# Between two stages of a three-block transformer kernel: where the next weights are split, how the last tiles are normed, and where the gate row and the meta tokens stand

## The reference

```python
# block 0 and 1 (the mixer is attention+convolution in 0, a 2-D Fourier transform in 1)
u = layer_norm(h) * (1 + sc1) + sh1
y = mixer(u) @ w_out
h = layer_norm(ALPHA * h + g1 * y) * ln_g[0] + ln_b[0]
u = layer_norm(h) * (1 + sc2) + sh2
h = layer_norm(ALPHA * h + g2 * (relu(u @ w1)**2 @ w2)) * ln_g[1] + ln_b[1]
# block 2 (16 learned meta tokens ahead of the 1024)
h = concat([meta_tokens, h])
h = h + mixer2(rmsnorm(h) * g) @ w_out_2
h = h + relu(rmsnorm(h) * g @ w_up)**2 @ w_down
return (rmsnorm(h) * final_g)[16:]
```

## Time and profile before

| | before |
|---|---|
| median of 3 runs | 3486.8 us (3484.27, 3486.8, 3490.0) |
| the profiled execution | 3484.21 us, span 3482.0 us, 2.2 us outside the span |
| mean granted TensorE clock | 0.958 of full speed |
| PE matmul busy | 3177.9 us, 91% of the span |
| DVE, ACT, POOL busy | 2156.8 us (62%), 1387.6 us (40%), 1074.6 us (31%) |
| chain that ended last | PE 72%, DVE 15%, ACT 8%, issue 3%, DMA 1% |

### The profile page before, as it was taken

The page is one execution under the profiler, slowest core; times in us unless marked ns, Lnnn a source line. Parts: engine busy times, 40 slices in busy tenths (PEclk is TensorE's granted clock), DMA queues, the critical chain, the costliest instruction groups (busy, mean ns, idle before and its releaser), DMA issues.

```text
span 3482.0 us, 36701 instructions
## 1 busy us (share of the span) xinstructions
PE 3177.9 (91%) x14623; PEld 2620.0 (75%) x14623; DVE 2156.8 (62%) x2795; ACT 1387.6 (40%) x1951; POOL 1074.6 (31%) x485
## 2 busy tenths in 40 slices
PE   7999888779999999869799999997985899999997
PEld 3888777668888888667588888886864678888886
DVE  4624677565777776775565666656776665555554
ACT  4311687344333333341533333335355353333332
POOL 0001464134444441322243344411580022222220
PEclk9999999989999999989899999998987899999999
DMA  6435211211233332110111111121120011111111
GB/s 220 141 128 159 77 55 35 85 42 61 98 103 103 102 102 75 33 37 19 43 55 49 55 49 49 49 67 32 37 92 18 25 55 60 50 61 49 55 55 55
DMA packets 190996, 237.86 MB, mean 68 GB/s; under 512 B 9672, under 2 KB 149563, under 8 KB 190827
## 3 DMA queue, kind: packets, MB, share of 16 engines
q1 hardware_dynamic: 173338, 172.90, 15.9%
q0 software_dynamic: 9136, 32.22, 2.5%
q10 hardware_dynamic: 8352, 30.41, 2.4%
HBM read 218.70 MB, written 16.79 MB: 68 GB/s over the span
## 4 chain that ended last, share of the span: by engine, by line
PE 72%; DVE 15%; ACT 8%; issue 3%; DMA 1%; SPq 0%; POOL 0%; DVEq 0%; ACTq 0%; POOLq 0%
PE psum L607 23%; PE psum L608 23%; PE psum L609 23%; DVE small L738 2%; DVE page_r L618 2%; DVE small L1367 2%; ACT temp L909 2%; DVE H L1472 1%; ACT U_hi L613 1%; DVE PT_lo L618 1%; DMA page<-in_ada_w_dram 1%; ACT prob L1333 1%; ACT page_r L613 1%; PE psum L899 1%; DVE small L763 1%
## 5 line engine op out<-in xcount | busy, mean ns | idle before, releaser
L607 PE MATMUL psum<-U_hi,page_r 128*128 128x512 f32 x2108 | 837.3, 397 | 62.6 <-DVE page_r L618 39.0
L608 PE MATMUL psum<-U_lo,page_r 128*128 128x512 f32 x2108 | 830.1, 394 | 0.0
L609 PE MATMUL psum<-U_hi,page_r 128*128 128x512 f32 x2108 | 829.3, 393 | 0.0
L618 DVE TENSOR_TENSOR page_r<-page,page_r 128x1024 fp32r<-128x1024 f32 (+2 forms) x239 | 350.9, 1475 | 371.9 <-ACT page_r L613 369.5
L607 PEld LDWEIGHTS psum<-U_hi,page_r 128*128 128x128 f32 x2108 | 402.0, 191 | 156.9 <-DVE page_r L618 42.8
L613 ACT CAST page_r<-page 128x1024 fp32r<-128x1024 f32 (+2 forms) x323 | 336.7, 1047 | 400.3 <-DVE page L638 110.1
L1972 ACT ACTIVATE temp<-psum 128x512 f32<-128x512 f32 x192 | 114.7, 598 | 884.6 <-PE psum L609 840.5
L609 PEld LDWEIGHTS psum<-U_hi,page_r 128*128 128x128 f32 x2108 | 401.6, 191 | 85.3
L608 PEld LDWEIGHTS psum<-U_lo,page_r 128*128 128x128 f32 x2108 | 402.3, 191 | 81.6
L607 PE MATMUL psum<-page_r,act_page_r 128*128 128x512 f32 x1176 | 457.5, 389 | 0.0
L608 PE MATMUL psum<-page_r,act_page_r 128*128 128x512 f32 x1176 | 457.5, 389 | 0.0
(11 more groups left out here) (344 smaller groups left out, 4849.7 us busy)
## 6 DMA issues: line engine op xcount, KB each, us to landing
page<-in_mlp_w_dram SPq DMA_DIRECT2D x128, 512.0 KB, 4.1
page<-in_ada_w_dram SPq DMA_DIRECT2D x48, 512.0 KB, 4.9
page<-in_w_in_dram SPq DMA_DIRECT2D x38, 512.0 KB, 4.1
page<-in_w_up_dram SPq DMA_DIRECT2D x32, 512.0 KB, 4.1
page<-in_w_down_dram SPq DMA_DIRECT2D x32, 512.0 KB, 4.3
ada_land<-in_ada_w_dram ACTq DMA_DIRECT2D x24, 512.0 KB, 4.4
sum_page<-in_ada_w_dram ACTq DMA_DIRECT2D x12, 512.0 KB, 5.5
act_page<-in_ada_w_dram ACTq DMA_DIRECT2D x12, 512.0 KB, 8.6
```

Of the source, the lines that this page charges most:

```text
L607: pe.matmul(out, l_hi, r_hi, start=start, stop=False, skip_group_check=read_between)
L608: pe.matmul(out, l_hi, r_lo, start=False, stop=False, skip_group_check=read_between)
L609: return pe.matmul(out, l_lo, r_hi, start=False, stop=stop, skip_group_check=read_between)
L618: return dve.tensor_tensor(lo, src, hi.bitcast(F32), ALU.subtract).then_inc(*k.lo.inc(*key))
```

## The change

It has six parts. (1) `place_mlp_unit`: u1, u2, u3 of an MLP's block 0 land in pages 0, 1, 2 and not in their slots' lo pages. d0 to d2, which land in the same pages, now wait for the splits of u1 to u3. (2) The splits of those weights (and of weights 2 to 4 of the projection behind `post3`), which stood behind or ahead of the whole late norm chain, are spread through it: `units(1)`, `units(2)`, `units(3)`. (3) The norm of tiles 6 and 7 in the four boundaries with a post norm is two steps on DVE, (h - mean) * g and then * scale + b, with no ACT instruction; the first of them for tile 6 and the second measuring of tile 5 move among the `U_lo` of chunk 0. (4) The gate rows (0,1) and (1,1) move from the MLP's block 0 to the place between the two halves of the output product before it, and all gate rows use a spread tile with four eighths side by side, so that DVE no longer waits for PE between eighths. (5) Two steps on one element per partition (L745 and L763) become `tensor_scalar` with per-partition scalars, from `scalar_tensor_tensor` with two tensors. (6) The norm of the meta tokens moves ahead of the projection's first tile, their transposes behind (3,0).

```diff
@@ place_mlp_unit
-        u.page = lo
-        u.raw = self.page[:, lo].rearrange("p a n -> p (a n)")
-        u.left_by = left[lo]
+        early = what == "u" and blk == 0 and j > 0
+        u.page = j - 1 if early else lo
+        u.raw = self.page[:, u.page].rearrange("p a n -> p (a n)")
+        u.left_by = left[u.page]
+        if early:
+            left[u.page] = [("taken", u)]
@@ dve_gate_row
     on.wait_ge(*k.lo.now())
+    if (layer, which) != (0, 0):
+        on.wait_ge(*k.gate_turned.at(*((layer, 0) if which else (layer - 1, 1)), KT - 1))
     for i in range(KT):
-        if i >= 2:
-            on.wait_ge(*k.gate_turned.at(layer, which, i - 2))
-        dve.tensor_scalar(k.temp[3 + i % 2][:, 0:P], k.ones[:], k.mod[:, layer, col + i:col + i + 1], None,
-                          ALU.mult).then_inc(*k.gate_spread.inc(layer, which, i))
+        dve.tensor_scalar(k.temp[3 + i // 4][:, (i % 4) * P:(i % 4 + 1) * P], k.ones[:],
+                          k.mod[:, layer, col + i:col + i + 1], None, ALU.mult).then_inc(
+            *k.gate_spread.inc(layer, which, i))
@@ dve_measure, dve_scale
-        m = dve.scalar_tensor_tensor(s[0:rows, 13:14], s[0:rows, 12:13], s[0:rows, 12:13], s[0:rows, 13:14], ALU.mult,
-                                     ALU.add)
+        m = dve.tensor_scalar(s[0:rows, 13:14], s[0:rows, 12:13], s[0:rows, 12:13], s[0:rows, 13:14], ALU.mult, ALU.add)
-        m = dve.scalar_tensor_tensor(s[:, 14:15], s[:, 12:13], -1.0, s[:, 15:16], ALU.mult, ALU.mult)
+        m = dve.tensor_scalar(s[:, 14:15], s[:, 12:13], s[:, 15:16], -1.0, ALU.mult, ALU.mult)
@@ pe_mix_out (and the same in pe_fourier; spreads and copies on DVE and ACT to match)
+    pe_gate_row(k, pe, on, 0, 1)
     for tt in range(TT):
         pe_down_tile(k, pe, on, "mix1", tt, units[FB:], lambda j, tt: u_operands(k, 4, j, tt),
@@ class Boundary
+    def late_units(self, k, n):
+
+        if self.name == "post3":
+            at = k.first["in2"]
+            return {1: (), 2: (at + 2,), 3: (at + 3, at + 4)}[n]
+        return (k.first[{"post0": "mlp0", "post2": "mlp1", "pre4": "mlp2"}[self.name]] + n,)
@@ act_boundary, at the last tile
+    units(1)
+    if b.rows:
+        act_root(k, act, on, P, b.name, "post", TT - 1)
+        act_root(k, act, on, P, b.name, "pre", TT - 3)
+        units(2)
+        act_root(k, act, on, P, b.name, "pre", TT - 2)
+    for t in range(TT - 3 if not b.from_u else TPC, TT - 1):
+        hat(t)
+    act_root(k, act, on, P, b.name, "pre", TT - 1)
+    hat(TT - 1)
+    if not b.rows:
+        units(2)
+    units(3)
@@ dve_boundary
+    def gain(t):
...
+        dve.scalar_tensor_tensor(h, h, mean, k.row_g[:], ALU.subtract, ALU.mult).then_inc(*k.step.inc())
+        on.wait_ge(*k.step.now())
+        dve.scalar_tensor_tensor(h, h, scale, k.row_b[:], ALU.mult, ALU.add).then_inc(*k.dve_gained.inc(b.name, t))
...
+    def between(i):
+
+        if b.rows and i == 0:
+            gain(TT - 2)
+        if b.rows and i == 4:
+            measure("pre", TT - 3)
...
+    units(1)
+    if b.rows:
+        measure("post", TT - 1)
+        units(2)
+        measure("pre", TT - 2)
+        scale("post", TT - 1)
+        gain(TT - 1)
+        scale("pre", TT - 3)
+        scale("pre", TT - 2)
+    measure("pre", TT - 1)
+    hat(TT - 3)
+    scale("pre", TT - 1)
+    hat(TT - 1)
+    if not b.rows:
+        units(2)
+    units(3)
@@ pe_mixers
         if (m, c) == (3, 0):
+            pe_boundary_rest(k, pe, on, b)
+        if (m, c) == (0, 1):
             on.wait_ge(*k.hat_ok.at("meta"))
```

More of the change, by code:

```diff
@@ L547, in place_mlp_unit @@
         self.parts_at(u, hi, lo)
-        u.before = [("product", (name, blk - 1), "6")] if blk and (what, j) == ("u", 1) else left[hi]
+        u.before = [("product", (name, blk - 1), "6")] if blk and (what, j) == ("u", 1) else left[hi] + (left[lo] if early else [])
         left[hi] = left[lo] = [("done", u.s)]
@@ L1515, in act_mix_out @@
         act_weights(k, act, on, k.first["mix"] + n)
+    act_gate_row(k, act, on, 0, 1)
     for tt in range(TT):
         act_boundary(k, act, on, BOUNDARY[0], tt)
-    for n in range(9, 12):
-        act_weights(k, act, on, k.first["mix"] + n)
 def dve_mix_out(k, dve, on):
@@ L1658, in turn, with units @@
             hat(old)
-    turn(tt)
+    def units(n):
+        for s in b.late_units(k, n):
+            act_weights(k, act, on, s)
+    if tt < TT - 1 or b.fourier:
+        turn(tt)
     if tt == TT - 2 and b.fourier:
@@ L1681, in dve_boundary, with measure, scale, hat @@
 def dve_boundary(k, dve, on, b, tt):
+    def gain(t):
+        h = k.H[:, t, :]
+        mean, scale = k.small[:, k.smalls.of(b.name, "post", t), 12:13], scale_bias(k, P, True, b.name, "post", t)[0]
+        on.wait_ge(*k.scaled.at(b.name, "post", t))
+        on.wait_ge(*k.row_g_in.at(b.name))
+        on.wait_ge(*k.row_b_in.at(b.name))
+        dve.scalar_tensor_tensor(h, h, mean, k.row_g[:], ALU.subtract, ALU.mult).then_inc(*k.step.inc())
+        on.wait_ge(*k.step.now())
+        dve.scalar_tensor_tensor(h, h, scale, k.row_b[:], ALU.mult, ALU.add).then_inc(*k.dve_gained.inc(b.name, t))
+    def measure(which, t):
+        if which == "pre":
+            on.wait_ge(*b.gained(k, t))
+        else:
+            on.wait_ge(*k.h_added.at(b.down, t, 1))
+        dve_measure(k, dve, on, k.H[:, t, :], P, D, b.rms if which == "pre" else False, b.name, which, t)
+    def scale(which, t):
+        dve_scale(k, dve, on, P, b.rms if which == "pre" else t >= TT - 2, b.name, which, t)
+    def hat(t):
+        if b.held_back(t) and b.on_vector(t):
+            s, bias = scale_bias(k, P, b.rms, b.name, "pre", t)
+            b.place_free(k, on, t)
+            on.wait_ge(*k.scaled.at(b.name, "pre", t))
+            dve.tensor_scalar(b.place(k, t), k.H[:, t, :], s, bias, ALU.mult, ALU.add).then_inc(*k.dve_hat.inc(b.name, t))
     def turn(n):
@@ L1998, in act_mlp @@
                     act_weights(k, act, on, s)
-            if tt == TT - 1 and not tile_first:
-                for s in ahead[1:]:
-                    act_weights(k, act, on, s)
             after(tt)
-        for s in ahead[1:] if tile_first else ():
+        for s in ahead[1:] if name == "mlp0" else ():
             act_weights(k, act, on, s)
@@ L2101, in dve_mlp @@
             dve_down_tile(k, dve, on, stage, tt, 1.0, ready)
-            if tt == TT - 1 and not tile_first:
-                for s in ahead[1:]:
-                    dve_weights(k, dve, on, s)
             after(tt)
-        for s in ahead[1:] if tile_first else ():
+        for s in ahead[1:] if name == "mlp0" else ():
             dve_weights(k, dve, on, s)
@@ L2406, in dve_fourier @@
         for tt in range(TT):
+            if not half and tt == TT - 2:
+                dve_gate_row(k, dve, on, 1, 1)
             dve_down_tile(k, dve, on, f"fout{half}", tt, 1.0 if half else ALPHA, ready)
@@ L2409, in dve_fourier @@
                 dve_boundary(k, dve, on, BOUNDARY[2], tt)
-        for s in range(at + 5 + 4 * half, at + 9 + 3 * half):
+        for s in range(at + 5, at + 9) if not half else ():
             dve_weights(k, dve, on, s)
@@ L2737, in act_out2 @@
         act_boundary(k, act, on, BOUNDARY[4], tt)
-    for s in range(at + 9, at + 12):
-        act_weights(k, act, on, s)
 def dve_mixers(k, dve, on):
```

140 lines of the change are left out of this document (62 added, 78 removed).

## The result

The changed kernel takes 3407.0 us (median of four runs, 3406.41 to 3411.5) against 3488.4 us of the kernel before in the same session: ratio 0.9776, interval 0.9763 to 0.9788, so 78 us faster by the ratio. The forecast was 3434 us, with 3413 us for rival B and a range from 3405 to 3455. The time lies inside the range, but near its lower end, and rival B comes closer than the forecast. The profiled execution of after is the slowest of its four (3411.5 us, span 3409.4), that of before the fastest of its runs, so the two traces are 72.6 us apart.

A forecast was written before the change was run, and what follows sets the result against it. It took TensorE's waits, chiefly 15.8 us for u1's split at post0 and post2, and the low clock behind them as the bound; 35 + 3 + 8.1 + 5 + 1 = 52 us off 3484.2 gave 3432, stated as 3434 us, range 3405 to 3455.

The forecast's parts named there:

- rival B: Norm's one-element steps run free of POOL at post0 to post3, together 20 us more gain, 3413 us; chance 0.27.
- I take the hold as staying: Norm's one-element DVE step, 1.75 us beside POOL's sum, was assumed to stay held as tensor_scalar.
- the 35 of the sum: post0 and post2: removing the u1 and gate row waits gains 17.5 us each, 35 us for both.
- the 3 us for gate rows: Two gate rows that stay, before attention and mlp0's last product, lose the DVE-PE hand-over: 1.5 us each.
- the charge of 2.9 us for the low clock: post0 and post2: PE idles about 8 of 11.7 us before (3,0), so 2.9 us is taken off 20.4.
- The order inside that sum: post0: u1, u2 split between measurings, tile 7's gains behind POOL's product, last hat, u3's copy, three up tiles, then (3,0).
- pre4: u1's split comes 0.4 us behind (0,0) in place of 6.0, then (1,0), (2,0) at full clock: 8.1 us gained.
- post3: New order from tile 7's add to (3,0) takes 24.5 us against 34.5; less low clock and meta wait, 5 us gained.
- The 1.9 us of PE's wait for the meta tokens' split: post3: the meta tokens' transposes behind (3,0) make PE wait about 1.9 us for their split.
- C: Scattered PE waits keep the clock low at three places, 17 us less gain, 3451 us; chance 0.15.
- E: Slower: u3's late split delays d2, d3 and POOL's sums for the block's products, about 3500 us; chance 0.04.
- D: Nothing: u1 to u3 land no earlier, leaving only the norm's and gate rows' parts; chance 0.02.

The follow-up runs named there:

- e1: Changed kernel with the two one-element steps of the norm written as scalar_tensor_tensor again: 3425.8 us, ratio 0.9828 to the kernel before.
- e2: Kernel before with only the two one-element steps turned into tensor_scalar: 3468.0 us, ratio 0.9950 to the kernel before.
- e3: Changed kernel with u1, u2, u3 in their old pages and all three split behind the last hat: 3425.9 us, ratio 0.9827.
- e6: Changed kernel with the meta tokens' norm, transposes and split ahead of (3,0) again: 3407.7 us, ratio 0.9773.
- e4: Changed kernel with u1, u2, u3 kept in the new pages but all split behind the last hat: 3425.4 us, ratio 0.9827.
- e8: Changed kernel with u3's copy behind u2's, gate row (1,0) spread earlier, meta tokens measured and rooted ahead of post3's last two weights: 3397.4 us, 0.9741.

## Why the prediction came out as it did

**The step that failed** is "I take the hold as staying". The small step of one element is not held beside POOL (0.21 us against 1.75), and e1 and e2 give it 18.5 and 17.5 us, near the 20 us of rival B. By stage, forecast of B against the table (after less e1): post0 3.7 and 3.9, post2 3.7 and 4.0, post3 some 6 and 6.8, post1 6 and 4.5. The mechanism of B and its places were right, and its prices to within 1.5 us; only the chance was too low. The nearest row that I had, four elements held for 1.15 us, was not near enough: two elements are held, one is not.

That the total comes so close to B's is in part luck. The order of the work gave 46.0 us at post0 and post2 in e1, 11 more than the 35 of the sum. Against that stand -2.0 us behind post0 and -6.8 in the second mixer, which no forecast had, and most of the 3 us for gate rows, which did not come.

**post0 and post2**: 22.0 and 24.0 us in e1, where the hold is there as the forecast had it, against 17.5. At post0 I had (3,0) at 774.8, 20.4 us earlier than before, and e1 has it 22.0 us earlier, counted from the same mark. The rest of the 4.5 us is the charge of 2.9 us for the low clock: e1 pays it behind (3,0), not before it (the clock is at 0.81 in the 12 us there, and the next stretch is 2.4 us longer). In the profile of after the clock was at 1.00 from 763 to 782, but at 0.79 in the 12 us behind (3,0) of post2. The 2 us more at post2 come from ahead of tile 7: in after PE's clock is at 0.92 there in post0 and at 1.00 in post2. I had called the two stages equal since the program is the same.

**The order inside that sum** was right: tile 7's gain steps beside POOL's product, the turn of u1, u2 and the measurings, the last hat, u3's copy and three relus, the turn. The wait for u1 is 0.45 us, (3,0) comes 32.0 us behind tile 7 where 32 to 34 were named (32.3 in e1; the prediction's own sum, with tile 7 2.4 us earlier and (3,0) at 774.8, would have said 35.2), and POOL's products start ahead of the last hat. The collision with POOL, for which the sum had two products of 2.4 us (d0 and d1), costs 0.6 us; that of d2 and d3 draws two `U_lo` to 3.49 us and then makes PE wait 0.37 us three times.

**The gate rows** cost nothing between the output products: the wait for the fifth weight in the mixer went from 2.89 to 1.10 us, and the next product starts at the same distance as before. For the two that stay I took 3 us for the lost hand-over. Their first waits are what they were, 3.27 us at (1,0) (3.28 before) and 0.55 before attention. From the row's first matmul to the next product it is now 3.1 us in place of 3.8 at (1,0) and 3.9 in place of 5.5 before attention; but 235 us further on only 0.1 us of the latter is left. So of the 3 us some 0.8 came.

**pre4**: 7.8 us measured, 8.1 forecast. **post3**: 6.6 us in e1 against 5. The forecast had a wait of 6.5 us for the banks that the sigmoids free, and it is 6.64. The 1.9 us of PE's wait for the meta tokens' split did not come: PE has no wait at all in the 50 us behind (3,0). **The second mixer** takes 6.8 us more in this trace, which the forecast didn't have; its mean granted clock is 0.84 in it and 0.87 in the trace of before.

**Rivals.** C is not what happened in full, but its mechanism is there in pieces: -2 us behind post0, -6.8 us in the second mixer. E needed POOL's sums of weights late; POOL's first sum of weights started 17.1 us behind (3,0) (787.24), 15.5 before, and PE's list shows no wait for it. D is out: u1 and u2 are copied at 746.54 and 751.55, and e3 loses 18.5 us.

What the parts are worth by taking one back at a time: small steps 18.5, weights 18.5, gate rows 17 to 20, norm in two steps 9 to 11, meta tokens 0. They sum to some 63 to 68 of 78 us. The rest is shared between parts or belongs to the order of VectorE's steps, which wasn't taken back by itself; which of the two is not shown.

## What to carry to other kernels

When an engine's wait names the last of a chain (here the split of u1), price the removal by the whole stretch up to the next point that all orders share. The wait at post0 was 13.3 us in e3, its removal gave 10.8, because the hats were the next to be late; and where two works each give PE a wait of 13 us in the same stretch (weights and gate row), moving one alone leaves the wait of the other. Look for short instructions that take ten times as long in one place as elsewhere: a change of form in two lines gave a quarter of this gain. After a change, read again which engine waits just before it does late work; here three such places gave another 10 us.

## What the runs showed of the hardware

- A VectorE `tensor_scalar` of one element to a partition takes 0.15 to 0.28 us whether POOL works or not; with two or three elements it is held up to 2.17 us, as was `scalar_tensor_tensor` with one element and two tensors in SBUF (up to 2.05 us before). By the Trainium skill (SBUF — State Buffer, Who interferes with whom, with VectorE: DVE Perf Modes, Mode 2×_2P) `tensor_scalar` can take the port pair that it shares with GpSimd when the outermost non-unit dimension is even, or odd and equal in source and destination. The traces agree: two and three elements meet that condition and are held. One element leaves no such dimension, and it is not held. Read without the word "non-unit" the condition would seem to take in one element too; the traces rule that reading out.
- The second mixer's stretch, with nearly the same work, took 320.1 us before, 320.8 in e6, 321.9 in e3, 323.6 in e1, 325.2 in e4, 326.3 in e8 and 326.9 in after, at mean granted clocks of 0.87, 0.87, 0.86, 0.86, 0.85, 0.85 and 0.84. In the piece shown above it is 0.50 or 1.00 for the same matmuls. What sets it there stays open. e3 and e4 have the same program in this stretch, so 3 us of it come and go without a change in its instructions, and a saving of 3 us ahead of it can't be read from one trace.
